# The sample rows' solver between halves of the projection's last products; the state in another buffer; first tile's turns ahead of the state products

## The reference

```python
p_mla, p_rwkv, p_conv = _split(h @ w_in, [MLA_PROJ, RWKV_PROJ, CONV_PROJ])
...
def step(s, inp):                      # RWKV-7, per head, state s is 64 x 64
    r_t, w_t, k_t, v_t, kk_t, a_t = inp
    sa = jnp.einsum('bhvk,bhk->bhv', s, -kk_t)
    s = (s * w_t[:, :, None, :] + sa[..., None] * (kk_t * a_t)[:, :, None, :]
         + v_t[..., None] * k_t[:, :, None, :])
    return s, jnp.einsum('bhvk,bhk->bhv', s, r_t)
```

## Time and profile before

| | us |
|---|---|
| median of 3 runs | 2940.8 |
| lowest and highest run | 2925.01 and 2943.41 |
| the profiled execution, its own time | 2958.15 |
| its span, first to last instruction | 2956.3 |
| busy in the span: PE | 2681.3 (91%) |
| DVE | 1359.5 (46%) |
| ACT | 798.9 (27%) |
| POOL | 648.3 (22%) |

### The profile page before, as it was taken

The page is one execution under the profiler, slowest core; times in us unless marked ns, Lnnn a source line. Parts: engine busy times, 40 slices in busy tenths (PEclk is TensorE's granted clock), DMA queues, the critical chain, the costliest instruction groups (busy, mean ns, idle before and its releaser), DMA issues.

```text
span 2956.3 us, 56002 instructions
## 1 busy us (share of the span) xinstructions
PE 2681.3 (91%) x22234; PEld 1472.1 (50%) x22234; DVE 1359.5 (46%) x3828; ACT 798.9 (27%) x1905; POOL 648.3 (22%) x664
## 2 busy tenths in 40 slices
PE   7999899999999959999599988999999996799996
PEld 4445566666655523333244456666666554233332
DVE  4212767666643542222441247677665536222224
ACT  0110355555532001111101014555555210011113
POOL 1000111111100035555310001111111000555543
PEclk9999799999999969999799988999999997899998
DMA  7213233333242539998751133333322326599985
GB/s 298 72 34 111 73 125 104 103 99 94 83 150 82 231 131 359 369 362 307 259 203 44 43 103 105 123 97 118 99 91 84 142 72 255 199 344 357 354 308 206
DMA packets 171814, 502.23 MB, mean 170 GB/s; under 512 B 48388, under 2 KB 89608, under 8 KB 146344
## 3 DMA queue, kind: packets, MB, share of 16 engines
q1 hardware_dynamic: 105624, 321.28, 31.5%
q0 software_dynamic: 50240, 120.23, 11.9%
q10 hardware_dynamic: 15696, 57.15, 4.8%
HBM read 629.15 MB, written 86.89 MB: 242 GB/s over the span
## 4 chain that ended last, share of the span: by engine, by line
PE 78%; DVE 9%; ACT 3%; another core or an unknown queue 3%; DMA 3%; issue 2%; DVEq 2%; POOL 0%; POOLq 0%; ACTq 0%; SPq 0%
PE ps L962 70%; PE ps L959 8%; ACT PT L1910 1%; DVE S_all L2942 1%; DVE grams L2458 1%; DMA xd<-o_x 1%; DMA c_x<-xd 1%; ACT S_all L2179 1%; DVEq L2943 1%; DMA l_b<-ybd,dga 0%; DVE krT L2965 0%; DVE negm L2944 0%; DVE uu L2458 0%; DVE t L2458 0%
## 5 line engine op out<-in xcount | busy, mean ns | idle before, releaser
L962 PE MATMUL ps<-w_slots,xbT 128*64 128x512 f32 (+1 forms) x2048 | 460.9, 603 | 19.0 <-DVE xbT L3419 19.0
L962 PE MATMUL ps<-hT,w_in 128*128 128x512 f32 x896 | 390.6, 594 | 1.2 <-ACT hT L1910 1.2
L962 PEld LDWEIGHTS ps<-w_slots,xbT 128*64 128x64 f32 x2048 | 144.6, 139 | 290.0 <-issue 270.7
L866 POOL DMA_INDIRECT xb<-xd,idall x256 | 256.1, 1001 | 144.7 <-issue 81.0
L962 PEld LDWEIGHTS ps<-hT,w_in 128*128 128x128 f32 x896 | 168.3, 190 | 206.1 <-issue 202.9
L3419 DVE STREAM_TRANSPOSE xbT<-xb 128x1024 f32<-128x1024 f32 x64 | 79.7, 1245 | 356.2 <-DMA xb<-xd,idall 348.7
L962 PE MATMUL ps<-w_slots,hidT 128*64 128x512 f32 (+1 forms) x1024 | 233.0, 593 | 9.6 <-issue 7.8
L962 PE MATMUL ps<-w_out,o_mixT 128*128 128x512 f32 (+1 forms) x640 | 238.3, 552 | 1.3 <-DVE o_h L3225 1.3
L962 PE MATMUL ps<-grams 64*64 64x64 f32 (+1 forms) x3536 | 147.0, 230 | 33.6 <-DVE grams L2458 25.4
L1910 ACT ACTIVATE kT<-ps 128x512 f32<-128x512 f32 x256 | 138.5, 593 | 127.6 <-PE ps L959 127.6
L962 PE MATMUL ps<-kcat,qcat 96*128 96x512 f32 (+3 forms) x384 | 151.7, 504 | 8.4 <-DVE negm L2944 8.4
(11 more groups left out here) (438 smaller groups left out, 4140.6 us busy)
## 6 DMA issues: line engine op xcount, KB each, us to landing
w_slots<-in_w_gu SPq DMA_DIRECT2D x64, 2048.0 KB
w_slots<-in_w_dn SPq DMA_DIRECT2D x64, 1024.0 KB
ybd<-yb ACTq DMA_DIRECT2D x64, 512.0 KB
pd<-stage SPq DMA_DIRECT2D x56, 256.0 KB, 2.4
w_in<-in_w_in SPq DMA_DIRECT2D x6, 2048.0 KB, 25.4
out_y<-c_h ACTq DMA_DIRECT2D x18, 512.0 KB, 2.8
o_mixT<-mixd SPq DMA_DIRECT2D x18, 512.0 KB, 3.8
xd<-o_x ACTq DMA_DIRECT2D x18, 512.0 KB, 3.1
```

The costliest lines, as they stand in the source:

```text
L866: pool.indirect_dma_start(xb[p % 2][:, 256 * q:256 * q + 256], None, x_quarters, bass.IndirectOffsetOnAxis(ap=idall[:, NE * q + p:NE * q + ...
L962: return pe.matmul(out, lhsT, rhs, start=start, stop=stop, skip_group_check=True)
```

## The change

sample_tile is gone from PE, ACT and DVE. Its steps stand in project: on PE between the halves (4 of 8 accumulated steps) of F1.6, F1.7 and M4 to M7; on ACT and DVE between the copies of these products. With them come ssq and th of tile 0 (ACT) and sg, ssx, kk and rows of tile 0 (DVE). PE's first_slot begins with mlaT and lora of tile 0, and u_sample comes behind them. DVE's first_slot has kkx and logs of tile 0 ahead of the sample's u_sample. stS lies in vrow[:, 2:4] and sel in PT[:, 0]; stS is loaded behind the store of the last feature and has its own semaphore. SP's other DMAs and POOL's list are not changed. The lists of marks are reordered to match (left out below, as are the places where a wait for window_in goes from 32 to 16).

```diff
-        stS = PT[:, 0].rearrange("p k t -> p (k t)").rearrange("p (b f v) -> p b f v", b=NB, f=2)
-        swr, sel = vrow[:, 1, 0:128].rearrange("p (f c) -> p f c", f=2), vrow[:, 2:4, :].rearrange("p f (b v) -> p f b v", b=NB)
+        stS = vrow[:, 2:4, :].rearrange("p f t -> p (f t)").rearrange("p (b f v) -> p b f v", b=NB, f=2)
+        swr, sel = vrow[:, 1, 0:128].rearrange("p (f c) -> p f c", f=2), PT[:, 0].rearrange("p k t -> p (k t)").rearrange("p (f b v) -> p f b v", f=2, b=NB)
...
+                    if n == NF - 1:
+                        sp.dma_start(stS, a["stS"][l].rearrange("p (b f v) -> p b f v", b=NB, f=2)).then_inc(stS_in, 16)
...
                 sp.wait_ge(pe_m.sem, pe_m.at(("proj", l), "M7"))
-                sp.dma_start(stS, a["stS"][l].rearrange("p (b f v) -> p b f v", b=NB, f=2)).then_inc(window_in, 16)
                 sp.dma_start(window[:], a["window"]).then_inc(window_in, 16)
...
-            def feature(l, g, f):
+            def feature(l, g, f, half=None):
                 n = AT[g, f]
-                if n >= 2:
+                if half != 1 and n >= 2:
...
-                for k in range(8):
+                for k in steps[half]:
                     m = mm(bank[4 + n % 2], w_in[:, k, MLA + f * P:MLA + f * P + P], hTg[g][:, k, :], k == 0, k == 7)
+                if half == 0:
+                    return
                 m.then_inc(pe_m.sem, pe_m.mark(("proj", l), f"F{g}.{f}"))
...
-            def latent_rows(l, t):
-                if t == 5:
+            def latent_rows(l, t, half=None):
+                if half == 1:
+                    pass
+                elif t == 5:
...
-                for k in range(8):
+                for k in steps[half]:
                     lhsT = hTg[t // 4][:, k, t % 4 * P:t % 4 * P + P] if t < NPT else hTs[:, k, :]
                     m = mm(bank[6 + t % 2][:W, 0:MLA], lhsT, w_in[:, k, 0:MLA], k == 0, k == 7)
+                if half == 0:
+                    return
                 m.then_inc(pe_m.sem, pe_m.mark(("proj", l), f"M{t}"))
...
-                feature(l, 1, 6)
-                feature(l, 1, 7)
-                for t in range(4, NPT):
-                    latent_rows(l, t)
+                feature(l, 1, 6, 0)
+                y.tokm()
+                feature(l, 1, 6, 1)
+                y.gramD()
+                feature(l, 1, 7, 0)
+                y.gram23()
+                feature(l, 1, 7, 1)
+                y.new()
+                y.sq(0)
+                y.gram4()
+                latent_rows(l, 4, 0)
+                y.rr(0)
+                y.sq(1)
+                latent_rows(l, 4, 1)
+                y.rr(1)
+                y.sq(2)
+                latent_rows(l, 5, 0)
+                y.rr(2)
+                latent_rows(l, 5, 1)
+                y.off1()
+                latent_rows(l, 6, 0)
+                y.off2()
+                y.mv()
+                latent_rows(l, 6, 1)
+                y.off3()
+                latent_rows(l, 7, 0)
+                y.wt()
+                latent_rows(l, 7, 1)
...
                 def new(self):
+                    pe.wait_ge(dve_m.sem, dve_m.at(("proj", self.l), "F1.6"))
                     pe.wait_ge(act_a.sem, act_a.at(self.k, "qlat"))
...
                 def u_sample(self):
-                    pe.wait_ge(window_in, 32 * (self.l + 1))
+                    pe.wait_ge(stS_in, 16 * (self.l + 1))
                     pe.wait_ge(act_a.sem, act_a.at(self.k, "wt"))
                     pe.wait_ge(dve_a.sem, dve_a.at(self.k, "new"))
...
-            def sample_tile(l):
-                x = Tile(l, NPT)
-                x.tokm()
-                ...
...
             def first_slot(l):
                 y, x, z, b = Tile(l, NPT), Tile(l, 0), Tile(l, 1), Sample(l, 0)
-                y.u_sample()
                 x.mlaT()
                 x.lora()
+                y.u_sample()
                 y.values_sample()
                 x.kks()
...
                 y.qn()
                 conv_feature(l, 1, 13)
                 y.qlat()
-                for t in range(4, NPT):
-                    latent_rows(l, t)
+                x = Tile(l, 0)
+                y.tokm()
+                y.sq(0)
+                y.sq(1)
+                latent_rows(l, 4)
+                x.ssq()
+                y.sq(2)
+                latent_rows(l, 5)
+                x.th()
+                y.off1()
+                y.off2()
+                y.mv()
+                latent_rows(l, 6)
+                y.wt()
+                latent_rows(l, 7)
...
-            def sample_tile(l):
-                x = Tile(l, NPT)
-                x.tokm()
-                x.sq(0)
-                y = Tile(l, 0)
-                y.ssq()
-                x.sq(1)
-                y.th()
-                x.sq(2)
-                x.off1()
-                x.off2()
-                x.mv()
-                x.wt()
...
                 y.qrT()
                 shift_feature(l, 1, 6)
+                y.conv_sample()
+                y.gramD()
+                y.gram23()
+                y.sq(0)
+                y.gram4()
                 shift_feature(l, 1, 7)
-                y.conv_sample()
+                y.new()
+                y.rr(0)
+                y.sq(1)
+                y.rr(1)
+                y.rr(2)
+                x = Tile(l, 0)
+                x.sg()
+                x.ssx()
+                x.kk()
+                y.off1()
+                y.off2()
+                y.off3()
+                x.rows()
+                y.wt()
...
             def first_slot(l):
                 y, x, z, b = Tile(l, NPT), Tile(l, 0), Tile(l, 1), Sample(l, 0)
-                x.rows()
+                y.z()
+                dve.wait_ge(pe_m.sem, pe_m.at(("proj", l), "M7"))
                 y.vm()
-                y.z()
+                x.kkx()
+                x.logs()
                 y.u_sample()
                 y.um()
-                x.kkx()
-                x.logs()
                 x.qn()
                 x.qr()
                 y.y_sample()
```

More of the change, by code:

```diff
@@ L191 @@
 PE_S = ("q kkb qlat qrT tokm gramD gram23 new sq0 gram4 rr0 sq1 rr1 sq2 rr2 off1 off2 mv off3 wt").split()
-PE_S0 = ("1u0 2mlaT 2lora 2kks 2q 2kkb 2kn 1y2 1st0 2V 2qrT 2tokm 2gramD 2gram23 2sq0 2gram4 2rr0 2sq1 2rr1 2sq2 2rr2 2off1 1mixT 2off2 2mv 2off3 2wt "
+PE_S0 = ("2mlaT 2lora 1u0 2kks 2q 2kkb 2kn 1y2 1st0 2V 2qrT 2tokm 2gramD 2gram23 2sq0 2gram4 2rr0 2sq1 2rr1 2sq2 2rr2 2off1 1mixT 2off2 2mv 2off3 2wt "
          "2u0 2st0 2u1 2st1").split()
 ACT_A = "2sq0 1mixT 2sq1 2sq2 2off1".split()
-ACT_S = "exps qn qlat tokm sq0".split()
-ACT_S0 = "2ssq 1sq1 2th 1sq2 1off1 1off2 1mv 1wt 2lora 2gate 2mlaT 2exps 2qn 2kn 2V 2qrT 2tokm 2sq0 2sq1 2sq2 2off1 1mixT".split()
+ACT_S = "exps qn qlat tokm sq0 sq1".split()
+ACT_S0 = "2ssq 1sq2 2th 1off1 1off2 1mv 1wt 2lora 2gate 2mlaT 2exps 2qn 2kn 2V 2qrT 2tokm 2sq0 2sq1 2sq2 2off1 1mixT".split()
 DVE_A = "1hnx 2gramD 2gram23 2sq0 2gram4 1yn 2rr0 2sq1 2rr1 2rr2 2off1".split()
-DVE_S = ("qn qr kk2 rkv qrT conv gramD gram23 new sq0 gram4 rr0").split()
-DVE_S0 = ("2ssx 1sq1 1rr1 2sg 2kk 1rr2 1off1 1off2 1off3 1wt 2rows 1vm 1z 1u0 1um 2kkx 2logs 2qn 2qr 1y 1st0 2kk2 2rkv 2kn 1hnx 2gramD 2gram23 2sq0 "
+DVE_S = ("qn qr kk2 rkv qrT conv gramD gram23 sq0 gram4 new rr0 sq1 rr1 rr2").split()
+DVE_S0 = ("2sg 2ssx 2kk 1off1 1off2 1off3 2rows 1wt 1z 1vm 2kkx 2logs 1u0 1um 2qn 2qr 1y 1st0 2kk2 2rkv 2kn 1hnx 2gramD 2gram23 2sq0 "
           "2gram4 2rr0 2sq1 2rr1 2rr2 1yn 2off1").split()
@@ L348, in build @@
         x0_in = [sem(f"x0_in{t}") for t in range(3, TILES)]
-        lnr_in, state_in, w_mix_in, window_in = (sem(n) for n in ("lnr_in", "state_in", "w_mix_in", "window_in"))
+        lnr_in, state_in, w_mix_in, window_in, stS_in = (sem(n) for n in ("lnr_in", "state_in", "w_mix_in", "window_in", "stS_in"))
         w_in_s = [sem(f"w_in_s{j}") for j in range(5)]
@@ L955, in _ @@
             halves = [slice(0, 64), slice(64, 128)]
+            steps = {None: range(8), 0: range(4), 1: range(4, 8)}
             def tr(out, in_, w=P):
@@ L1555, in seam @@
                 b.v(3)
-            def sample_tile(l):
-                x = Tile(l, NPT)
-                x.tokm()
-                x.gramD()
-                x.gram23()
-                x.new()
-                x.sq(0)
-                x.gram4()
-                x.rr(0)
-                x.sq(1)
-                x.rr(1)
-                x.sq(2)
-                x.rr(2)
-                x.off1()
-                x.off2()
-                x.mv()
-                x.off3()
-                x.wt()
             def first_slot(l):
                 y, x, z, b = Tile(l, NPT), Tile(l, 0), Tile(l, 1), Sample(l, 0)
-                y.u_sample()
                 x.mlaT()
                 x.lora()
+                y.u_sample()
                 y.values_sample()
@@ L1897, in _ @@
                 project(l)
-                sample_tile(l)
                 first_slot(l)
@@ L2938, in s @@
                     if h == 0:
```

(29 more changed lines are left out.)

7 lines of the change are left out of this document (removed).

## The result

The changed kernel takes **2949.7 us** (median of 20 runs, 2942.6 to 2961.3) against 2938.8 for the kernel before in the same comparison (20 runs, 2924.9 to 2943.4): a ratio of **1.0044, 95% interval 1.0033 to 1.0056**, so 12.9 us more (9.7 to 16.5) by the ratio, which is taken over all runs; the two medians differ by 10.9. 2947 had been forecast, from +6.2 us. The profiled execution took 2947.64 us (span 2945.8). It is shorter than the profiled one of before (span 2956.3), so the two are not compared as wholes but step by step. For that I take the start of the same instruction in both traces and subtract what they differ by already ahead of the change (0.41 us later in after), or ahead of layer 1's stretch (6.13; o_rows' product at 1693.96 for 1687.82).

What follows compares the result with a forecast made beforehand. PE was taken to bound the kernel (78% of the chain), with DVE the bound just ahead of tile 0. Tile 0 starting 3.1 us later in each of two layers gave 2940.8 + 6.2 = 2947 us, bounds 2945 to 2963.

Steps and rivals of the forecast that it cites:

- Step 1: Sample solver placed between the projection's products: solver 10.1 us, breaks 1.0, M7 ends at 290.5 us, no stall in the tail.
- The breaks: Splitting products around the solver: about fourteen breaks at some 0.07 us each, 1.0 us per layer, upper end 1.8.
- Step 2: Behind M7, tile 0's root waits behind the page gathers: x.rows done at 301.5 us, PE idle from 290.5.
- Step 3: Tile 0's turns in first_slot: kks done at 309.5 us, rkv at 328.2, tile 0 starts 3.1 us later.
- the list: DVE's work in first_slot from kkx on, with u_sample and um, up to rkv: 18.7 us.
- st's wait: DVE's wait of 0.97 us for st in first_slot falls away, as PE is far ahead.
- Nothing takes the delay up: Behind tile 0's start the code is the same, so the 3.1 us delay stays in each layer, +6.2 us.
- Step 4: Sampled rows' state in its new place, with stS loaded earlier: the load is hidden and costs nothing.
- The unknown stalls: Waits on an unknown queue while the gathers run, now during x.rows and mlaT: 0 to 3 us per layer, taken as zero.
- A: Root behind the gathers does not bind: mlaT starts at 290.5 us, -9.0 us per layer, 2923 us; chance 0.12.
- B: Clock falls inside the tail, at DVE's queue before rr1: tile 0 starts 20 us late, 2981 us; chance 0.07.
- C: Gain and loss cancel: root sooner after M7, full clock earlier, three us less per layer, 2941 us; chance 0.11.

Runs made afterwards that it cites:

- e8: Kernel before, with two useless 32 by 32 products ahead of each half of the projection's last six products: 2966.5 us, ratio 1.0032.
- e1: Changed kernel with tile 0's row_root ahead of the first page gathers on POOL, and a wait for M7's copy in values_sample: 2930.7 us, ratio 0.9903.
- e6: Changed kernel with 15 useless products given to PE in its wait behind M7: 2962.9 us, ratio 1.0009 to the kernel before.
- e5: Kernel before with only the sampled rows' state in its new home, loaded early on its own semaphore: 2957.3 us, ratio 0.9993.
- e4: Kernel before with only tile 0's row_root moved ahead of the first page gathers on POOL: 2952.0 us, ratio 0.9974.
- e7: e1 with key_root of tile 0 also ahead of the first gathers on POOL: 2937.8 us, ratio 0.9926 to the kernel before.
- e9: e7 with kks ahead of the sampled rows' values product on PE: 2919.6 us, ratio 0.9933 to the kernel before.
- e3: e1 with first_slot's PE and DVE orders of the kernel before (u_sample first; u_sample and um ahead of kkx): 2935.9 us, ratio 0.9913.
- e10: e1 with kks ahead of the sampled rows' values product on PE: 2913.8 us, ratio 0.9921 to the kernel before.

## Why the prediction was right

**Step 1, the tail: right, one term too small.** M7 ended at net 290.9 for 290.5. PE had no wait in the tail, and DVE reached rr1 in time. The solver cost 9.5 us beside the products, not 10.1. The breaks cost 2.0 us, not 1.0 (half features 0.4, half latent products 20.6 - 18.93 = 1.7), which is above my upper bound of 1.8. I had taken the price from two whole products and one alone. PE's timeline of before on both sides of the one alone:

```profile
237.30 1.97 PE L962 MATMUL ps<-o_rows,grams 64*128 64x32 f32 x16
...
246.26 0.40 PE L959 MATMUL ps<-cst,o_rows 32*32 32x32 f32 x8
```

It does stand between products of other tile sizes, and from start to start it takes 7.07 us where half of the two in a row is 6.92: 0.15, near the 0.17 to 0.20 of e8. The slip was to halve the 0.13 "for the two ends": each cut makes one more piece, and each piece pays the whole. Twelve places at 0.17 make the 2.0. (The lower bound for M7 should read 289.5, not 289.4; nothing hangs on it.)

**Step 2, the root behind the gathers: right.** First gather 3.3 us after M7 (3.4 forecast), root done 10.2 after it (10.4), rows scaled at net 301.8 (301.5), PE idle 11.0 us. e1 confirms it by removing the cause.

**Step 3, tile 0's turns: right in kind, 1.2 us too small.** Layer 0's +4.3 for +3.1 is 0.3 from the rows, 0.45 from the turns and 0.4 from the list, with rounding. The full clock was forecast 5.2 us after PE resumes, and came after about 4.8 (0.50 until 306, then 0.86 on average until 310, so full from about 307.1). What was mis-sized is mlaT and lora with the gate: I took 2.7 us from before, where their later part ran at full clock already, and here all of it ran at half, 3.7 us. u_sample, at half clock only to begin with, took 2.4 where I had 3.0. Together 8.4 us from rows to kks for 8.0; e1 and e6 need 6.2. And st's wait did not fall away wholly: the state product ran at half clock (3.67 us), DVE waited 0.40 for it, and the list took 19.1 for 18.7.

**"Nothing takes the delay up" behind tile 0: not borne out in this trace.** In layer 0 the delay grew from net 4.3 to 6.5 us at the start of tile 2 and was 5.2 at that of tile 7; in layer 1 it shrank from 4.7 to 1.5 and then to -0.1. Together 5.1 us are left where I had 6.2. But executions with the same order move as much there: by tile 7 of layer 0 e5 is net 6.2 behind before, in layer 1 0.4. The runs say 12.9 (9.7 to 16.5), and the 5 to 11 us beyond the trace's 5.1 I can't place: the expert stages, whose code is the same, differ by up to 17 us between two executions.

**The number: close in part by luck.** 2947 is 2.7 us from 2949.7, but the kernel before came out 2.0 us lower (2938.8 for 2940.8), and the change cost 10.9 us by the medians or 12.9 by the ratio, about twice the 6.2 of the sum. The sign and the step that costs the time were right; the size was low.

**Step 4, the home: right** (e5). **The unknown stalls: right to take at zero**, but probably for another reason than mine: in e4 they seem to follow the gathers, and here the gathers ran while PE and DVE stood still anyway.

**Rivals.** A did not happen, but its price for tile 0 holds: with the root first it starts 9.0 us earlier in layer 0, the figure forecast, as kks came sooner (6.2 us after M7 for 6.9) and DVE's list took longer (19.3 for 18.7). For the whole kernel A's 18 us were too few: e1 won 20 to 38. B: the clock was 1.00 to M7's end. C: the root came no sooner after M7. The clock did matter, but behind the wait and not in the tail, where B had it.

## What to carry to other kernels

When work is moved off the front of a queue, look at every queue that was ordered for the old time: a root of 0.7 us that had been hidden for 12 us came to stand in front of the whole core, and swapping two lines made 1.4% (1.0044 to 0.9903). Price an idle array at more than its length, since the clock is lower behind it. Price the longest chain through all engines after a change, not the wait that was removed: of four further rearrangements none made the timed kernel shorter than e1, though in layer 1 two of them brought tile 0 forward by some 1.9 us. And don't read 3 to 6 us off two single traces: executions with the same order differed by that much here.

## What the hardware showed

**A break in the array's tile size costs 0.17 to 0.20 us** in e8, and down to 0.07 beside some neighbours in after (3.53 for 3.46). The Trainium skill (TensorEngine Tiling (Array Packing), Key Properties) says that changing the mode drains the array; the cost in e8 fits that and gives it a size, though no trace shows the drain itself.

**An idle array loses more than its idle time.** Behind 10.8 us without an instruction the granted clock was 0.50 (1.2 GHz) from 302.2 to about 307. With products of no use in the hole it stayed 1.00 up to 310, kks came 2.2 us sooner after the rows, and the timed ratio fell from 1.0044 to 1.0009. A long hole isn't needed for a fall: in e1 PE waits at most 1.76 us between M7 and 302, and its clock is 0.55 from 302 to 306 and 0.50 from 306 to 310.

**A gather's issue waits for a DVE product of two tensors in SBUF.** A gather's issue takes 0.94 to 0.96 us on POOL (the first of a group 1.18). In e7 it took 2.41, beside DVE's 2.28 us product (the rows of e7 above); it ended at 306.32, 0.82 us after DVE's at 305.50. In e9 2.61 us, and again 0.82 after DVE's end; in e3 2.38 us and 0.83. Layer 1 of the three has the same: 2.65 to 2.69 us, ended 0.82 to 0.84 after DVE. No other gather in them took over 1.25 us. Beside DVE instructions with one input in SBUF they took no longer than ever: 0.95 beside a reduction of 1.91 us in e7, 0.94 and 0.95 beside products with a PSUM input in e10. The Trainium skill (SBUF — State Buffer, SBUF: two separate sides) tells of an exclusive lock on a port pair, which a VectorE instruction with two inputs in SBUF holds against a GpSimd instruction that reads SBUF. The three kernels agree with it, if the gather's reading of its offsets from SBUF is such a read, which no run tests.
